# Another order of the lanes beside the second block's projections, GELU from the exponential, output tiles earlier

## The reference

```python
x = first_block(x, ...)       # attention + conv + gated merge, then a gated MLP of 2816, RMS norm
h = x @ w_in_2                # 17 slices: NSA q/k/v/gates/z, stick-breaking q,k,v,z, HGRN2 q,f,i,z
o_nsa = nsa_mixer(...)        # 6 heads: compressed, selected, window branches
#   compress: gelu(blocks @ w1) @ w2, for a key and a value source
o_sb = stick_breaking_mixer(q, k, v)   # 4 heads
#   z = q k^T * scale;  r = log_sigmoid(-z) under the strict mask; rcs = reverse cumsum of r
#   a = exp(log_sigmoid(z) + rcs shifted) under the mask;  o = a @ v
o_hg = hgrn2_mixer(q, f, i, lb)        # 6 heads, gated linear recurrence, here by log2 levels
x = layer_norm(ALPHA * x + concat(o_nsa * silu(z1), o_sb * silu(z2), rms(o_hg) * w * silu(z3)) @ w_out_2)
```

## Time and profile before

| | us |
|---|---|
| median of 3 runs | 1102.44 |
| lowest, highest | 1100.87, 1102.79 |
| profiled execution | 1101.64 |
| its span | 1099.4 |
| PE, DVE, ACT busy in it | 1063.4, 619.1, 451.4 |
| mean granted clock of TensorE | 0.994 of 2.4 GHz |

### The profile page before, as it was taken

One profiled execution on the slowest core, in us unless ns is written; L12 is line 12 of the kernel. 1 busy time (PEld: TensorE's weight loads), 2 busy tenths in 40 slices (PEclk: granted clock), 3 DMA queues, 4 the chain that ended last, 5 costly groups with the idle time before them and its releaser, 6 DMA issues.

```text
span 1099.4 us, 13928 instructions
## 1 busy us (share of the span) xinstructions
PE 1063.4 (97%) x5454; PEld 850.1 (77%) x5454; DVE 619.1 (56%) x1167; ACT 451.4 (41%) x825; POOL 27.4 (2%) x41
## 2 busy tenths in 40 slices
PE   6999999999999999999999999999998899999997
PEld 5877778888879888888888888988776686666575
DVE  5457654445355666532666634445685673566657
ACT  5344333232254444421343434543345456556640
POOL 0000000000011000000000000200000001000000
PEclk9999999999999999999999999999999999999999
DMA  7421123323332832341332233242111123310011
GB/s 264 154 78 58 58 77 96 96 96 96 118 115 74 298 106 89 118 129 55 96 96 96 96 124 125 92 144 80 57 56 49 39 87 98 151 56 27 16 58 77
DMA packets 29103, 107.06 MB, mean 97 GB/s; under 512 B 3226, under 2 KB 3370, under 8 KB 28400
## 3 DMA queue, kind: packets, MB, share of 16 engines
q1 hardware_dynamic: 24288, 84.04, 23.3%
q0 software_dynamic: 4032, 19.96, 5.2%
q10 hardware_dynamic: 720, 2.20, 0.5%
HBM read 101.44 MB, written 7.36 MB: 99 GB/s over the span
## 4 chain that ended last, share of the span: by engine, by line
PE 88%; DVE 6%; ACT 3%; issue 2%; DMA 1%; ACTq 0%; DVEq 0%; SPq 0%
PE ps L671 25%; PE ps L673 24%; PE ps L672 24%; PE ps L1050 2%; PE ps L1084 1%; PE ps L1067 1%; PE ps L945 1%; PE ps L811 1%; DVE wlo L1482 1%; PE ps L784 1%; PE ps L1017 1%; PE ps L796 1%; ACT whi L1149 1%; DMA XT<-xt 1%; PE ps L982 1%
## 5 line engine op out<-in xcount | busy, mean ns | idle before, releaser
L671 PE MATMUL ps<-XH,whi 128*128 128x512 f32 (+1 forms) x864 | 338.8, 392 | 9.9 <-DVE wlo L1499 8.3
L673 PE MATMUL ps<-XH,wlo 128*128 128x512 f32 (+1 forms) x864 | 328.2, 380 | 0.0
L672 PE MATMUL ps<-XL,whi 128*128 128x512 f32 (+1 forms) x864 | 328.0, 380 | 0.0
L1482 DVE TENSOR_TENSOR wlo<-raw,whi 128x1024 fp32r<-128x1024 f32 (+1 forms) x158 | 189.3, 1204 | 182.1 <-ACT whi L1149 182.0
L671 PEld LDWEIGHTS ps<-XH,whi 128*128 128x128 f32 x864 | 163.6, 189 | 50.7 <-issue 18.3
L1149 ACT CAST whi<-raw 128x1024 fp32r<-128x1024 f32 (+1 forms) x158 | 161.2, 1026 | 85.9 <-PE ps L673 57.5
L673 PEld LDWEIGHTS ps<-XH,wlo 128*128 128x128 f32 x864 | 163.4, 189 | 31.4
L672 PEld LDWEIGHTS ps<-XL,whi 128*128 128x128 f32 x864 | 163.8, 190 | 27.7 <-issue 0.5
L671 PE MATMUL ps<-whi,GH 128*128 128x512 f32 x176 | 68.9, 391 | 0.0
L672 PE MATMUL ps<-wlo,GH 128*128 128x512 f32 x176 | 68.6, 389 | 0.0
L673 PE MATMUL ps<-whi,GL 128*128 128x512 f32 x176 | 68.5, 389 | 0.0
(11 more groups left out here) (275 smaller groups left out, 1346.6 us busy)
## 6 DMA issues: line engine op xcount, KB each, us to landing
raw<-wp SPq DMA_DIRECT2D x150, 512.0 KB, 3.5
vec_dram<-row_dram POOLq DMA_DIRECT2D x1, 3072.0 KB, 13.1
H<-x POOLq DMA_DIRECT2D x1, 2048.0 KB, 8.1
x_dram<-H POOLq DMA_DIRECT2D x1, 2048.0 KB, 7.6
A<-w1c POOLq DMA_DIRECT2D x2, 1024.0 KB, 6.6
A<-x_dram POOLq DMA_DIRECT2D x1, 2048.0 KB, 12.7
y<-A SPq DMA_DIRECT2D x8, 256.0 KB, 2.0
raw<-wp SPq DMA_DIRECT2D x4, 402.0 KB, 3.6
```

Of the source, the lines that this page charges most:

```text
L671: self.e.matmul(o, ah, bh, start=start, stop=False)
L672: self.e.matmul(o, ah, bl, start=False, stop=False)
L673: return self.e.matmul(o, al, bh, start=False, stop=stop)
L1482: self.e.tensor_tensor(wlo[BUF[i]][:, 0:w], raw[i % NR][:, 0:w], whi[BUF[i]][:, 0:w].bitcast(F), ALU.subtract).then_inc(sems["lo"], 1)
```

## The change

In the projections' stage: `h_q1` comes ahead of `h_diag`, and `h_prep(0)` moves one step later. `split_all` becomes two calls, `split_hi` (ScalarE, where `slot` was) and `split_lo` (VectorE, after the second quarter of the tile). The stick-breaking lane starts at turn 32 with one step per turn; VectorE's part of `s_first` becomes `s_soft`, one step later, and the masks of `s_second` become `s_mask`, at the next `s_first` or one step behind the last `s_second`. GELU (tanh form) is made of Square and Exp on ScalarE and six small VectorE instructions per source, x / (1 + exp(-c x (1 + 0.044715 x^2))), so that ScalarE stays in one table set; the two GELU loads and the two loads back go. The load of the exponential's set for the NSA stage moves ahead of the copy of `s_pv(1)`.

In the NSA stage: TensorE signals after each of three quarters of the last gate slot (`zx`), and `mix_tile(0..2)` are written beside that slot; the rest of `mix_tile` and the four `out2` come one turn or more earlier. Several semaphores are merged (`nsk` into `vev`, `kl0` into `one`, `dm` into `osm`), with counts shifted; these hunks are left out below, as are the other projections' loops, which are changed in the same way.

```diff
@@ -347,45 +349,57 @@

     def projections():
         for g in range(4):
-            slot(B2_V + g)
+            en.split_hi(B2_V + g + 3)
             for t in range(4):
                 en.av(g, t)
+                if t == 1:
+                    en.split_lo(B2_V + g + 3)
                 yield
         for i in range(2):
-            slot(B2_SQ + i)
+            en.split_hi(B2_SQ + i + 3)
             for part in range(4):
                 en.sq(i, part)
+                if part == 1:
+                    en.split_lo(B2_SQ + i + 3)
                 yield
...
     def hgrn():
         for p in range(3):
             en.h_start(p)
             yield
+            en.h_q1(p)
             en.h_diag(p)
-            en.h_q1(p)
-            en.h_prep(p, 0)
             yield
             en.h_off(p, 0)
+            en.h_prep(p, 0)
             en.h_prep(p, 1)
             en.h_mult(p, 0)
             yield
@@ -424,39 +438,48 @@
     def stick():
         for p in range(2):
             for n in range(4):
+                if n:
+                    en.s_mask(p, n - 1)
                 en.s_first(p, n)
                 yield
+                en.s_soft(p, n)
                 yield
                 en.s_second(p, n)
                 yield
+            en.s_mask(p, 3)
             yield
             en.s_pv(p)
             yield

-    weave(projections(), (hgrn(), 4, 45 / 54), (stick(), 33, 28 / 26), (compress(), 42, 14 / 16))
+    weave(projections(), (hgrn(), 4, 45 / 54), (stick(), 32, 1), (compress(), 42, 14 / 16))

     def gates():
         for n in range(8):
-            slot(B2_Z + n)
+            en.split_hi(min(B2_Z + n + 3, N_SLOTS))
             for part in range(4):
                 en.z(n, part)
+                if part == 1:
+                    en.split_lo(min(B2_Z + n + 3, N_SLOTS))
                 if n >= 4 and part == 1:
                     en.mix_mul(n - 4)
+                if n == 7 and part > 0:
+                    en.mix_tile(part - 1)
                 yield
         en.mix_mul(4)
-        en.mix_tile(0)
-        en.mix_tile(1)
+        en.mix_tile(3)
         yield
-        en.mix_tile(2)
+        en.out2(0, 0, 0)
+        en.mix_tile(4)
         yield
-        for g in range(2):
-            for t in range(2):
-                en.out2(0, g, t)
-                if g == 0 or t == 0:
-                    en.mix_tile(3 + 2 * g + t)
-                if g:
-                    en.mix_rows(t)
-                yield
+        en.out2(0, 0, 1)
+        en.mix_tile(5)
+        yield
+        en.out2(0, 1, 0)
+        en.mix_rows(0)
+        yield
+        en.out2(0, 1, 1)
+        en.mix_rows(1)
+        yield
         en.mix_rows(2)

     def nsa():
@@ -903,7 +928,9 @@
                 self.tile(B2_SK + i, part, 4, 2)

             def z(self, n, part):
-                self.tile(B2_Z + n, part, 4, 2)
+                f = self.tile(B2_Z + n, part, 4, 2)
+                if n == 7 and part < 3:
+                    f.then_inc(sems["zx"], 1)

             def h_diag(self, p):
                 q, k = HG[:, p, 0, :], HG[:, p, 1, :]
@@ -1153,6 +1180,8 @@
                 for i in range(self.splits, n):
                     self.split(i)

+            split_hi = split_all
+
             def begin_norm(self, m):
                 self.e.preload_act_table_set(SQRT)

@@ -1335,9 +1364,6 @@
             def sk(self, i, part):
                 self.bring(B2_SK + i, part, SK[:, i, :], "sk2")

-            def nsa_begin(self):
-                self.e.preload_act_table_set(EXP)
-
             def z(self, n, part):
                 if part == 3:
                     self.wait_ge("used", B2_Z + n + 1)
@@ -1385,8 +1411,10 @@
             def c_mm(self, i, part):
                 if part == 3:
                     self.wait_ge("cm", i + 1)
-                    self.e.activation(HC[:, i, :], ps[6][:, 0:62], ACT.Gelu_apprx_tanh).then_inc(sems["hc"], 1)
-                    self.e.preload_act_table_set(LNEXP)
+                    self.wait_ge("hc", 3 * i)
+                    self.e.activation(GE, ps[6][:, 0:62], ACT.Square).then_inc(sems["gx"], 1)
+                    self.wait_ge("gv", 3 * i + 3)
+                    self.e.activation(GE, GE, ACT.Exp, scale=-GELU).then_inc(sems["gx"], 1)

             def c_end(self):
                 self.wait_ge("kc", 1)
@@ -1441,13 +1469,18 @@
                     self.e.activation(AA[j][kb], ps[STICK[j]][:, kb * 128:S], ACT.Exp).then_inc(sems["s_e"], 1)

             def s_pv(self, p):
+                if p == 1:
+                    self.e.preload_act_table_set(EXP)
                 self.wait_ge("s_av", p + 1)
                 self.e.copy(OTS[:, 3 + p, :], ps[STICK[0]][:, :]).then_inc(sems["s_o"], 1)

             def mix_tile(self, n):
                 if n < 5:
                     self.wait_ge("t_m", n + 1)
-                    self.wait_ge("used", SLOT_WOUT2)
+                    if n // 2 < 3:
+                        self.wait_ge("zx", n // 2 + 1)
+                    else:
+                        self.wait_ge("used", SLOT_WOUT2)
                     self.e.copy(XH[:, n, :], OTS[:, n, :]).then_inc(sems["t_h"], 1)

             def mix_rows(self, qb):
@@ -1487,6 +1520,8 @@
                 for i in range(self.splits, n):
                     self.split(i)

+            split_lo = split_all
+
             def first_x(self, k):
                 self.wait_ge("pp", 16)
                 self.wait_ge("xh", k + 1)
@@ -1863,6 +1898,23 @@
                         sv = src.rearrange("p (m b k) -> p b k m", b=8, k=2)[:, :, j, a:a + 31]
                         pos = PO[r, 8 * a:8 * a + 8].rearrange("p (b o) -> p b o", o=1).to_broadcast([64, 8, 31])
                         self.e.tensor_tensor(BLK[r, 8 * a:8 * a + 8, g, :], sv, pos, ALU.add).then_inc(sems["blk"], 1)
+
+            def c_mm(self, i, part):
+
+                if part == 3:
+                    x = ps[6][:, 0:62]
+                    self.wait_ge("gx", 2 * i + 1)
+                    self.e.tensor_scalar(GE, GE, 0.044715, 1.0, ALU.mult, ALU.add).then_inc(sems["gv"], 1)
+                    self.wait_ge("gv", 3 * i + 1)
+                    self.e.tensor_tensor(GE, GE, x, ALU.mult).then_inc(sems["gv"], 1)
+                    self.wait_ge("gv", 3 * i + 2)
+                    self.e.tensor_scalar(GE, GE, -50.0, None, ALU.max).then_inc(sems["gv"], 1)
+                    self.wait_ge("gx", 2 * i + 2)
+                    self.e.tensor_scalar(GE, GE, 1.0, None, ALU.add).then_inc(sems["hc"], 1)
+                    self.wait_ge("hc", 3 * i + 1)
+                    self.e.reciprocal(GE, GE).then_inc(sems["hc"], 1)
+                    self.wait_ge("hc", 3 * i + 2)
+                    self.e.tensor_tensor(HC[:, i, :], GE, x, ALU.mult).then_inc(sems["hc"], 1)

             def n_qk(self, n):
                 qb, br, h = UNITS[n]
@@ -1898,7 +1950,7 @@
                                             SZT[:, 5:8, qb * 128:qb * 128 + 128], ALU.mult,
                                             ALU.mult).then_inc(sems["n_o"], 1)

-            def s_first(self, p, n):
+            def s_soft(self, p, n):
                 kb, at = 3 - n, 4 * p + n
                 cs = slice(kb * 128, S)
                 self.wait_ge("mc", N_MC)
@@ -1921,6 +1973,9 @@
                         self.wait_ge("s_r", 4 * p + 2 * (n - 2) + j + 1 if n > 1 else 0)
                         self.e.tensor_tensor(tail, tail, cols(SPb, j, kb + 1, kb * 128 + 128), ALU.add
                                              ).then_inc(sems["s_r"], 1)
+
+            def s_mask(self, p, n):
+                kb, at = 3 - n, 4 * p + n
                 for j in range(2):
                     diag = AA[j][kb][:, 0:128]
                     self.wait_ge("s_e", 2 * at + j + 1)
```

More of the change, by code:

```diff
@@ L51 @@
 C_N = C_ROW + 1
+GELU = 2.0 * (2.0 / np.pi) ** 0.5
 LEVELS = [64, 32, 16, 8, 4, 2, 1]
@@ L83 @@
 sq eps rt rs pg nlo nhi tr xh xl tm res
-qev vev nsk qk tt ex t1 cp av sk skx nrm ft ahi alo
+qev vev qk tt ex t1 cp av sk skx nrm ft ahi alo
 cvc cvp cvy cvt cvz cvh cvl gt bra bm ma mh ml
-vem dm ve lb lbe ua ub sl um gh gl
-fb fc hk sc one kl0 qz hq hv hgt avv src nk nq sq2 sk2 zc zt
+vem ve lb lbe ua ub sl um gh gl
+fb fc hk sc one qz hq hv hgt avv src nk nq sq2 sk2 zc zt zx
 h_d h_x h_e h_dg h_ta h_qk h_k2 h_of h_oc h_p h_pe h_m h_pr h_av h_sq h_rm h_ln h_rs h_ot blk1
-blk cm hc kc kct mc
+blk cm gx gv hc kc kct mc
 n_qk n_tt n_ex n_tr n_ca n_av n_cf n_sc n_o
@@ L167, in idle @@
         pass
-    begin = first = sums = roots = split = split_all = norm_rest = turn = part = fm = idle
+    begin = first = sums = roots = split = split_all = split_hi = split_lo = norm_rest = turn = part = fm = idle
     q = k = v = qk = soft = tr = cp = pv = fin = ft = cc = cx = cb = gate = branch = merge = wout = idle
@@ L174 @@
     c_move = c_blk = c_mm = c_end = begin_norm = block2_after = idle
-    n_qk = n_scale = n_tr = n_pv = n_out = nsa_begin = s_first = s_second = s_pv = mix_mul = mix_tile = mix_rows = last = out2 = end = idle
```

(17 more changed lines are left out.)

26 lines of the change are left out of this document (17 added, 9 removed).

## The result

The changed kernel takes 1095.1 us (median of 5 executions, 1093.33 to 1097.85) beside 1101.32 us for the kernel before on the same chip (5 executions, 1098.87 to 1102.79). The ratio is 0.9951 with an interval of 0.9937 to 0.9966: 5.4 us faster, between 3.7 and 6.9 (the two medians lie 6.2 apart). Forecast were 1097.2 us and a net gain of 5.2. The profiled execution has a span of 1095.5 us, 3.9 less than before.

The account below looks back on a forecast made before the run. TensorE, busy 1063.4 of 1099.4 us, bounds the kernel, so only its stands and half clock can be won back. Gains of 17.5 less losses of 12.3 give net 5.2: 1097.2 us, likeliest range 1094.5 to 1100.2.

Parts of the forecast that it names:

- Part 1: Pair starts beside the projections: `h_q1` ahead of `h_diag` makes K1 and K2 ready before `h_off`; gain 2.7 us.
- Part 2: Projections: VectorE's weight splits after the second quarter no longer wait for ScalarE's casts, shortening `h_prod` waits; gain 2.3 us.
- Part 3: Stick-breaking in three steps: later `s_soft` and masks remove stands and half clock in HGRN pair 2; gain 8.9 us.
- rival (d): Level turns: VectorE's work, not its waits, is the bound; slower, 1109 us, or 1105 at half effect; chance 0.11.
- The loss behind `c_blk`: `s_soft(1,1)` falls behind the second source's DMA-waiting `c_blk`; TensorE stands 4.9 us, a short `h_prod(6)` wait included.
- Part 4: GELU from the exponential: removed table loads worth nothing; chain hides in turn 48, delays `s_soft(1,3)` from turn 55; loss 2.8 us.
- Clock: Half clock after the new stands at `s_second(1,1)` (3.1 us) and `s_second(1,3)` (1.5); loss 4.6, bounds 0 and 6.8.
- Part 5: NSA's start: exponential's table loaded before `s_pv`'s copy, and the split no longer ahead of second-pair scores; gain 1.3 us.
- Part 6: NSA's end: XH and XL tiles written during the last gate slot, `out2` earlier; gain 2.3 us, bounds 0 and 4.
- (a): The new stands cost no clock, or the second hides; net 9 to 12 us, time 1092; chance 0.25.
- (b): `s_soft(1,1)` is not late because the DMA lands sooner; time under 1089.5 us; chance 0.06.
- (c): Levels: VectorE's waiting only moves, parts 1 and 2 give 1 instead of 5.0 us; 1101.2; chance 0.16.

Follow-up runs that it names:

- the good order: Changed kernel with c_blk(1,0) behind s_soft(1,1), second GELU behind s_soft(1,3), earlier second-source moves, first GELU in turn 49 ahead of stick-breaking: 1086.49 us.

## Why the prediction was right, and where it was not

The time came within 2.1 us and inside the likeliest case, but one large term of the sum was credited to the wrong edit, and one term was missing.

- **Part 1** (2.7): 1.37 us per pair is what the two `h_off` show with the old order, and 1.27 what starts give. Right. It is worth more than I gave it: with the old order, pair 2 also has the 3.12 us at `s_second(0,2)`, and the order by itself costs 4.6 us between the same instructions.
- **Part 2** (2.3): at the places that I named it is about right. The three stands of level products behind `h_pick` of over 0.5 us (1.03, 0.67 and 0.61 by starts) are gone, 2.3 together, and small ones of 0.2 to 0.35 stay, as worked. But as an edit it is worth far more: 4.2 us alone on the kernel before, 8.8 by medians in the good order. I had counted its waits at the picks only, not what else queues behind a VectorE that waits for a cast, nor the gates: NSA's first half won 1.8 us for which my sum had no term. The late splits are behind most of it: alone they give 1.7 there, and without them 1.2 are lost. One stand of 0.55 us by starts, ahead of the row at 962.59 in before, is part of that; the rest is too small a piece in each turn for me to assign.
- **Part 3** (8.9): the stands and the half clock in pair 2 did go, and the lead at `h_prod(5)`, 12.2 us, is not far from the 13.9 that parts 1 to 3 add up to (rival (d) has 14.1, a slip). The small stands that I had put against it are there too, 0.54 at `s_second(0,2)` and 0.49 at `h_prod(0)`. The reason was wrong. Undoing the delay of `s_soft` brings none of the large ones back. The failed step is "In pair 2 of HGRN this removes": I read the row at 849.72, VectorE waiting 2.69 us for the softplus, and took the pair of engines that it names for the cause. One row further back, ScalarE waits 4.41 us for VectorE, which is then at work on the diagonal products, Q1, K1, K2 and the preparation. The order of the pair's start removes that. What removes the 2.17 before L945 at 865.88 isn't settled. It is not the splits: with late splits alone it stays (2.34), and in the kernel with all but late splits that level product does not wait (the 2.06 there is at the next one, behind a split that waits for its cast). It is gone with the old order and `s_soft` late, and with the new order and `s_soft` early, so neither of these two is needed for it by itself. The later masks and the earlier start of the lane were undone by themselves in no run.
- **The loss behind `c_blk`** (4.9): right in place, cause and size, 3.82 and 1.11. But the 1.11 at `h_prod(6)` is there in every kernel with the first GELU chain in its place, `c_blk` moved or not (1.11 to 1.14), and gone in those with this chain a turn later or on ScalarE's table function. So it belongs to that chain, of which Part 4 says that it "hides". In the changed kernel this is true of the sum, for a TensorE that came sooner would have waited longer for `c_blk`; with `c_blk` moved it is a loss of its own. The order of `c_blk` costs 3.8. Issuing the moves earlier takes away 1.7 of it, another order all.
- **The loss behind GELU** (2.8): 3.14 by starts, with the stand at that place about 0.6 without the chain: 2.6. Right. The chain from 909.37 to `s_soft` at 911.31 took 1.9 us against my 2.3.
- **Clock** (4.6, bounds 0 and 6.8): 6.8. Both stands were paid with 3.4. The Trainium skill (TensorE: Matmul & The Clock Gate, HAM oscillation) pointed at the higher figure, 6.2 by my working, and this execution agrees with it; the kernel with `c_blk` behind `s_soft` does not, since there the same 3.14 us stand was followed by full clock.
- **Part 5** (1.3): 1.2. Right.
- **Part 6** (2.3): 1.9 against before in the two traces, and 1.9 between the same instructions when undone alone, though the medians don't show it. 1.7 of it is a half clock, which followed the stand of 2.17 in all three traces that have this stand.
- **Rivals.** (a) did not happen: the clock fell at both. (b): the stand is there. (c) and (d): from 758 to 800 us TensorE is busy 41.89 of 42 us with VectorE at 31.14; no level waits over 0.5 us up to `h_prod(5)` of pair 2, and VectorE is not the bound. It was busy 10.49 of 12 us from 850 to 862, 87%, and 26.36 of 32 from 851 to 883, 82%, not far from the 90% at which I had let (d) decide. Of (c) this much is true: VectorE's waiting moved in part, to `h_norm`.

The sum came out because the wrong credit still stood for a gain that the change as a whole makes. That it came so close is partly luck: parts 1 to 3 gave 1.7 less and the clock took 2.2 more than forecast, and the 1.8 in NSA stood in no term. Asked which edit to keep, it would have misled: Part 3, priced at +8.9 with 4.9, 2.8 and the clock against it, rests on the delay of `s_soft`, which shows nothing on its plus side, and without it the kernel runs at 1085.54 us, faster than the changed one.

## What to carry to other kernels

Before moving a step later on an engine that works in order, list what now stands ahead of it and what that work waits for; a wait for a DMA or for another engine's chain is passed on to everything queued behind, so such work goes behind what TensorE needs soonest. A row that says who released a wait gives one step only: follow it back until an engine was working rather than waiting, and credit the edit that touches that end. Splitting a change into its edits on the chip pays: here one edit alone (late splits) gave 4.2 us where the whole change gave 5.4, and taking another back made the gain more than twice as large. The worths do not add up (the same splits are worth 8.8 us among other orders), so an edit is best tried both alone and taken out of the whole.

## What the runs showed of the hardware

- The same stand of TensorE, 3.14 us at the same place, was followed by 6.8 us at the 1.2 GHz level in the changed kernel and by none in the kernel with `c_blk` moved. In the first the clock had been low some 20 us earlier (884.7 to 891.5), and so it had in the kernel with early moves (886.5 to 889.9, then 3.13 us of stand and low from 910.4 to 917.2); in the second it had not. That this is the reason was not tried. Stands of 3.12 and 3.16 us in two other kernels were followed by full clock too, the 2.06 before the second of these by a half clock of 1.7 us loss. Shorter ones of 2.14 (early moves) and 2.17 us (old tile places) had 3.4 us at the 1.2 GHz level. The length of a stand alone doesn't tell its price.
- Executions of one kernel differ by the clock: of the changed kernel's five, one has a span of 1091.1 us at a mean granted clock of 0.997, another 1095.5 at 0.993. 0.004 of 1093 us is 4.4, as much as the spans differ by.
- The two small moves from on-chip memory to on-chip memory land 2.2 us after issue for the first source, with nothing just ahead of them on the queue, and 2.4 and 3.4 us for the second when issued ahead of W1's load. With W1's megabyte issued just before, they took 5.8 and 5.9 us in the changed kernel, and up to 7.2 in the kernel before with late splits alone.
